# First mixer of a two-trunk network: attention scores emitted in pairs, gate decays interleaved with the last projection jobs, fills in other steps

## What is computed

```python
def trunk_layer(x, cx, c, c_ctx, ...):
    sh1, sc1, ga1, sh2, sc2, ga2 = modulation(c, w_mod, b_mod)       # silu(c) @ w_mod: 1024 x 6144
    u  = (rmsnorm(x,  g_mix) * (1 + sc1)  + sh1)  @ w_in             # 1024 x 2080
    uc = (rmsnorm(cx, g_mix) * (1 + sc1c) + sh1c) @ w_in             # context tokens, 256
    p, gq, gk, gv, gg, rf, rb, aq, ak, av = split_in(u)
    # gated linear attention, both directions, state carried context -> latent
    o_gc, s_f, s_b = gla_bidir(*gla_features(gqc, gkc, gvc, rfc, rbc, ...), 0, 0)
    o_gl, _, _     = gla_bidir(*gla_features(gq, gk, gv, rf, rb, ...), s_f, s_b)
    # softmax attention, 8 query heads of 64, 2 key heads
    #   latent queries see context + latent keys (512), context queries only context (256)
    mix = concat([pool_mixer(p), gla_output(o_gl, gg), latent_attention(ql, k_all, v_all)]) @ w_out
    x = x + ga1 * mix
    x = x + ga2 * squared_relu_mlp(rmsnorm(x) * (1 + sc2) + sh2, w_up, w_down)
    # the same for cx in layer 0 only

def gla_chunk_scan(...):   # the decays: S_new = exp(bl) * S + (k * exp(bl - b))^T v,  b = cumsum(la)
```

## Time and profile before

| what | us |
|---|---|
| median of three runs | 1911.78 |
| lowest, highest | 1906.54, 1918.8 |
| the profiled execution | 1916.42 |
| its span, first to last instruction | 1914.6 |
| mean granted TensorE clock | 0.942 of full |

### The profile page before, as it was taken

One profiled execution on the slowest core, in us unless ns is written; L12 is line 12 of the kernel. 1 busy time (PEld: TensorE's weight loads), 2 busy tenths in 40 slices (PEclk: granted clock), 3 DMA queues, 4 the chain that ended last, 5 costly groups with the idle time before them and its releaser, 6 DMA issues.

```text
span 1914.6 us, 25663 instructions
## 1 busy us (share of the span) xinstructions
PE 1761.6 (92%) x10636; PEld 1411.5 (74%) x10636; DVE 1072.7 (56%) x1634; ACT 704.2 (37%) x878; POOL 84.5 (4%) x87
## 2 busy tenths in 40 slices
PE   4999998899999998999889997987999979779998
PEld 1786456777777777764579995675999766669996
DVE  3664456554444445764566775555666464656654
ACT  2323345321313123433444444363433243633332
POOL 1020000100000001100000001000000010010000
PEclk9999887999999999998989998988999979889999
DMA  9325870224344334258545555431555553335542
GB/s 341 115 104 187 314 271 1 96 86 149 133 149 150 139 132 145 86 182 305 201 152 197 198 181 184 165 132 63 179 177 168 197 202 118 131 110 176 176 168 96
DMA packets 172371, 309.18 MB, mean 161 GB/s; under 512 B 3264, under 2 KB 54720, under 8 KB 171616
## 3 DMA queue, kind: packets, MB, share of 16 engines
q1 hardware_dynamic: 168592, 293.98, 43.8%
q10 hardware_dynamic: 3376, 12.00, 1.8%
q0 software_dynamic: 288, 1.57, 0.2%
HBM read 305.44 MB, written 2.10 MB: 161 GB/s over the span
## 4 chain that ended last, share of the span: by engine, by line
PE 77%; DVE 12%; ACT 4%; DMA 3%; issue 2%; POOL 1%; DVEq 0%; ACTq 0%; POOLq 0%; SPq 0%
PE bank L576 59%; PE twin L576 15%; DVE ring_r L1223 3%; PE bank L585 2%; ACT arena_r L1985 2%; DMA ring<-in_w_in 2%; DMA ring<-in_w_mod 2%; ACT arena L1985 2%; DVE arena L1223 1%; POOL rs L2396 1%; DVE params L1223 1%; DVE arena L1315 1%; DVE arena_r L1223 0%; DVE X L1733 0%; DVE actT_r L1318 0%
## 5 line engine op out<-in xcount | busy, mean ns | idle before, releaser
L576 PE MATMUL bank<-arena_r 128*128 128x512 f32 (+2 forms) x2128 | 702.0, 376 | 14.7 <-DVE arena_r L1855 6.7
L1223 DVE TENSOR_TENSOR ring_r<-ring,arena_r 128x4096 fp32r<-128x4096 f32 (+4 forms) x98 | 394.3, 4023 | 203.6 <-ACT arena_r L1985 202.8
L576 PEld LDWEIGHTS bank<-arena_r 128*128 128x128 f32 x2128 | 405.7, 191 | 94.7 <-issue 8.1
L1985 ACT ACTIVATE arena_r<-ring 128x4096 fp32r<-128x4096 f32 (+4 forms) x96 | 323.5, 3370 | 386.8 <-PE bank L576 129.8
L576 PE MATMUL twin<-actT_r,arena_r 128*128 128x256 f32 x1408 | 254.7, 284 | 1.1 <-DVE actT_r L1223 1.1
L576 PE MATMUL bank<-ring_r,arena_r 128*128 128x512 f32 x624 | 246.1, 394 | 0.0
L576 PE MATMUL bank<-arena_r,actT_r 128*128 128x512 f32 (+3 forms) x624 | 222.0, 387 | 11.9 <-DVE ring_r L1223 5.0
L1985 ACT ACTIVATE arena<-bank 128x512 f32<-128x512 f32 (+6 forms) x195 | 91.8, 471 | 360.8 <-PE bank L576 276.5
L576 PEld LDWEIGHTS twin<-actT_r,arena_r 128*128 128x128 f32 x1408 | 220.1, 192 | 1.7 <-DVE actT_r L1223 1.7
L576 PE MATMUL twin<-actT_r,ring_r 128*128 128x256 f32 x704 | 199.4, 283 | 0.0
L576 PE MATMUL bank<-ring_r,actT_r 128*128 128x512 f32 (+3 forms) x496 | 184.6, 372 | 0.0
(11 more groups left out here) (193 smaller groups left out, 1679.8 us busy)
## 6 DMA issues: line engine op xcount, KB each, us to landing
ring<-in_w_mod SPq DMA_DIRECT2D x24, 2048.0 KB, 9.2
ring<-in_w_ada SPq DMA_DIRECT2D x24, 2048.0 KB, 9.0
ring<-in_w_gate_up SPq DMA_DIRECT2D x44, 1024.0 KB, 7.7
ring<-in_w_down SPq DMA_DIRECT2D x20, 2048.0 KB, 7.9
ring<-in_w_up SPq DMA_DIRECT2D x16, 2048.0 KB, 7.8
ring<-in_w_in SPq DMA_DIRECT2D x12, 2048.0 KB, 11.0
ring<-in_w_out SPq DMA_DIRECT2D x8, 2048.0 KB, 11.2
ring<-in_w_down SPq DMA_DIRECT2D x8, 1792.0 KB, 7.6
```

What stands on the lines that cost most here:

```text
L576: ins = nc.tensor.matmul(out_, lhsT, rhs, start=start, stop=stop)
L1223: return v.tensor_tensor(o, x, y, op)
L1985: return nc.scalar.activation(o, x, func, **kw)
```

## The change

1. **Scores in pairs.** `scores1(l, i)` is called for even i only, and emits the matmuls of steps i and i+1 alternately, into two banks: first the two of head index 0, then, where the range is 256, the two of head index 1. In the loop it stands after `turned1(l, i)` instead of at the head of the step, for even i.
2. **Decays beside the jobs of chunk 4.** `decays(l, tiles)` is called after each of them, with one tile in layer 0 and two in layer 1. The order inside is turned round: the two matmuls of 256 columns first, then the four with one column of that tile. The one-column results go to a bank of ring `s`, and ScalarE takes their exponential after that of the last tile. VectorE multiplies a job later, and waits for ScalarE's last exponential before the mixer.
3. **Fills.** In layer 0 the steps of the fills are 0-5, 7, 8, 9, 11, 12, 13, 15, 17 instead of 0-13; in layer 1 0, 1, 2, 4, 5, 6, 8, 9, 11, 12 instead of 0-5, 8-11. In a step of `WEIGHTED1` the fill comes after `values1`, right ahead of `logs` and `gated_scores`. The number of fills and `loads()` stay. `sums` moves from step 17 to 20 and from 6 to 7. `mod_columns` keeps its steps (`n - 3` is 21 and 13).
4. **Pooling.** The two inner loops change places, so that neighbouring matmuls write different halves of the partitions.

```diff
+def decay_tiles(l, t):
+    return [t] if l < L - 1 else [2 * t, 2 * t + 1]
...
-WEIGHTED1, FILLS1 = [[1, 6, 11, 16], [1, 7]], [range(0, 14), (0, 1, 2, 3, 4, 5, 8, 9, 10, 11)]
-SUMS1, HALVES1 = [17, 6], [20, 12]
+WEIGHTED1 = [[1, 6, 11, 16], [1, 7]]
+FILLS1 = [(0, 1, 2, 3, 4, 5, 7, 8, 9, 11, 12, 13, 15, 17), (0, 1, 2, 4, 5, 6, 8, 9, 11, 12)]
+SUMS1, COLUMNS1, HALVES1 = [20, 7], [21, 13], [20, 12]
...
-            def decays(l):
-                b, filled = take("a")
-                for t in range(4):
-                    for j in range(4):
-                        mm(b[:, 4 * t + j:4 * t + j + 1], la[:, t, j * P:(j + 1) * P], const("up16")[:, P - 1:P],
-                           inc=filled if t == 3 and j == 3 else None)
-                for t in range(4):
+            def decays(l, tiles):
+                if tiles[0] == 0:
+                    pe.wait_ge(la_ready, nth(la_ready))
+                    mark["decs", l] = take("s")
+                whole, whole_filled = mark["decs", l]
+                for t in tiles:
                     b, filled = take("a")
                     mm(b[:, 0:256], const("after16"), la[:, t, 0:256])
                     mm(b[:, 256:512], const("before16"), la[:, t, 256:512], inc=filled)
-                mark["dec", l] = k["a"] - 4
+                    mark["dec", l, t] = k["a"]
+                    for j in range(4):
+                        mm(whole[:, 4 * t + j:4 * t + j + 1], la[:, t, j * P:(j + 1) * P],
+                           const("up16")[:, P - 1:P], inc=whole_filled if t == 3 and j == 3 else None)
...
             def scores1(l, i):
-                heads = steps1(l)[i]
-                b, filled = take("p")
-                for n, (p, e) in enumerate(heads):
-                    t, hp, k0 = pairs1(l)[p]
-                    mm(b[:, 256 * n:256 * n + 512 - k0], qT[64 * e:64 * e + 64, hp, t * P:(t + 1) * P],
-                       kT[64 * e:64 * e + 64, hp // 2, k0:512], inc=filled if n == len(heads) - 1 else None)
+                both = [(s_, take("p")) for s_ in (i, i + 1)]
+                for n in range(len(steps1(l)[i])):
+                    for s_, (b, filled) in both:
+                        heads = steps1(l)[s_]
+                        p, e = heads[n]
+                        t, hp, k0 = pairs1(l)[p]
+                        mm(b[:, 256 * n:256 * n + 512 - k0], qT[64 * e:64 * e + 64, hp, t * P:(t + 1) * P],
+                           kT[64 * e:64 * e + 64, hp // 2, k0:512], inc=filled if n == len(heads) - 1 else None)
...
                 scores1(l, 0)
-                scores1(l, 1)
                 fill()
                 fill()
                 for i in range(n + 1):
-                    if i + 2 < n:
-                        scores1(l, i + 2)
                     if i == 1:
                         pooling(l)
                     if i == 2:
                         pooled(l)
-                    if i in FILLS1[l]:
+                    if i in FILLS1[l] and i not in WEIGHTED1[l]:
                         fill()
                     if i < n:
                         turned1(l, i)
+                    if i % 2 == 0 and i + 2 < n:
+                        scores1(l, i + 2)
                     for p in ended(l, i - 1):
                         values1(l, p)
+                    if i in FILLS1[l] and i in WEIGHTED1[l]:
+                        fill()
...
-                    if j == jobs_until(l, 4):
-                        pe.wait_ge(la_ready, nth(la_ready))
-                        decays(l)
+                    if c == 4:
+                        decays(l, decay_tiles(l, t))
...
-                    if j == jobs_until(l, 4) + 1:
-                        decays(l)
+                    if c == 4 and t > 0:
+                        decays(l, decay_tiles(l, t - 1))
+                decays(l, [3] if l < L - 1 else [2, 3])
+                nth(s_filled)
+                dve.wait_ge(s_emptied, nth(s_emptied))
                 mixer1(l)
```

More of the change, by code:

```diff
@@ L813, in pooling @@
                     for s in range(n // S):
-                        for par_ in range(2):
-                            for t in range(2):
+                        for t in range(2):
+                            for par_ in range(2):
                                 end = s == n // S - 1 and par_ == 1 and t == 1
@@ L911, in mixer1 @@
                             gated_turned(l, t)
-                    if i == n - 3:
+                    if i == COLUMNS1[l]:
                         mod_columns(l + 1)
@@ L1420, in heads, with decays @@
                 dve.wait_ge(a_emptied, mark["qT", l, 1])
-            def decays(l):
+            def decays(l, tiles):
                 ke4 = VIEWS1[l][2]
-                for t in range(4):
-                    dve.wait_ge(a_emptied, mark["dec", l] + 1 + t)
+                for t in tiles:
+                    dve.wait_ge(a_emptied, mark["dec", l, t])
                     for d in range(2):
@@ L1576, in mixer1 @@
                         pooled(l)
-                    if i == n - 2:
+                    if i == COLUMNS1[l] + 1:
                         mod_columns(l + 1)
@@ L2083, in heads, with decays @@
                     step(f(qT[:, j, 0:n], b[:, 0:n], ACT.Copy), a_emptied)
-            def decays(l):
+            def decays(l, tiles):
                 ke4, dec = VIEWS1[l][2], VIEWS1[l][8]
-                b = filled()
-                step(f(dec, b[:, 0:16], ACT.Exp), a_emptied)
-                for t in range(4):
+                for t in tiles:
                     b = filled()
                     step(f(ke4[:, t, :], b[:, :], ACT.Exp), a_emptied)
+                if tiles[-1] == 3:
+                    nth(s_filled, 5)
+                    nth(s_emptied, 5)
+                    b = filled("s")
+                    step(f(dec, b[:, 0:16], ACT.Exp), s_emptied)
             def gated_heads(l):
@@ L2232, in layer1 @@
                     last_c = c
-                    if j == jobs_until(l, 4):
-                        decays(l)
-                nth(s_filled, 5)
-                nth(s_emptied, 5)
+                    if c == 4:
+                        decays(l, decay_tiles(l, t))
                 mixer1(l)
```

## The result

| | before | after |
|---|---|---|
| median of the runs | 1911.9 us (10 runs, 1906.2 to 1918.8) | 1897.8 us (10 runs, 1892.3 to 1903.9) |
| ratio, 95% interval | | 0.9928 [0.9912, 0.9943] |
| span of the profiled execution, its mean clock | 1914.6 us, 0.942 | 1902.1 us, 0.943 |

The change brings 14 us, 0.7%: faster by less than 1%. The prediction said 1894 (1883 to 1908). By the intervals the first set gives 10.9 to 16.8 us and the second 13.6 to 21.8. The forecast sum, 17.9 us, lies above the first and inside the second.

A forecast was written before the change was run, and what follows sets the result against it. TensorE was taken as the bound, busy 92% of the span, with waits and low clock in the mixers. Gains of 7.8 + 5.8 + 4.3 = 17.9 us from a 1911.8 us median gave 1894, range 1883 to 1908.

The forecast's parts named there:

- Decays, 3.9 us a layer: Decays of chunk 4: clock holds, 6.2 us instead of 10.4, less a short wait before `states`; 7.8 us in all.
- The rival that the clock falls all the same: Decays, or `logs` and `states` just after: clock still falls, decays give nothing, 1902 us; chance 0.12.
- Pairs, 1.05 us each: Scores in both mixers: two matmuls run side by side, each pair saving 1.05 us; 19.0 us of work.
- That they don't run side by side: Rival, scores in the loop: only the first pair overlaps, nothing saved and cover lost, 1913 us; chance 0.03.
- The walk of waits: Mixer steps: extra waits where scores no longer cover other engines' chains, 5.7 us in layer 0, 3.25 in layer 1.
- Pooling order, 0.2: Pooling in the mixers: the new order saves the lone first half-pair, 0.2 us a layer.
- Fills' transfers: Weight loads for moved fills in the mixers: no wait expected; otherwise one late landing, 1 to 3 us.
- The 0.4 us of waiting for a chunk in layer 1: First fill with weights issued inside layer 1's mixer: TensorE there at 10.4 us, weights at 10.8.
- Mixer of layer 0, 5.8 us: Layer 0: 11.6 from pairs plus 0.2 pooling less 5.7 of waits is 6.1, taken as 5.8 us gain.
- Mixer of layer 1, 4.3 us: Layer 1: 7.4 from pairs plus 0.2 pooling less 3.25 of waits, a gain of about 4.3 us.
- The clock rival: Both mixers: thinner work is granted less clock, 3.4 us per further low stretch, up to 1931 us; chance 0.04.
- The sign by the clock: Layer 0's mixer: forecast wrong if windows at 0.5 clock total much more or less than about 50 us.

The follow-up runs named there:

- decays_only: The kernel before with the interleaved decays alone, mixers as they were: 1903.1 us, ratio 0.9960 to before.
- lump: The changed kernel with all 16 one-column matmuls of a layer together after the last tile's 256-column matmuls: 1903.6 us, ratio 0.9957 to before.
- old_fills: The changed kernel with fills and sums at their old steps in both layers: 1901.2 us, ratio 0.9932 to before.
- new_fills_layer0: The changed kernel with fills and sums of layer 1 back at their old steps, layer 0 keeping the new: 1896.4 us, ratio 0.9920 to before.
- again: The changed kernel unedited, a second set of six runs with a second profile: 1897.3 us, ratio 0.9908 to before.
- dense_in_waits: The changed kernel plus 16 dense matmuls that nobody reads, put into its mixers' waits: 1894.4 us, ratio 0.9907 to before.
- both: The changed kernel with fills moved into waits and unread dense matmuls in the waits left: 1882.7 us, 0.9856 to before; repeated unchanged 1888.3 us, 0.9879.
- no_pairs: The changed kernel with one score matmul a step at its head, as before; new fills and decays kept: 1906.0 us, ratio 0.9977 to before.

## Why the prediction was right, and where not

The parts of the mechanism were found as forecast: cheaper decays by the clock, the price of a pair, and the places of the waits. That the sum came within 4 us of the median is in part chance, since the mixers' clock moves by several us from one execution to the next, and the sum took it as fixed.

- **Decays, 3.9 us a layer.** From the end of the first job of chunk 4, 139.25, to `logs`, 158.41, before took 19.16 us; after takes 15.55 (141.36 to 156.91). In layer 1 it went from 13.41 us (825.29 to 838.70) to 9.80 (818.30 to 828.10). That is 3.6 a layer, 7.2 in both, and 7.6 by the runs of `decays_only`. The small wait before `states`, forecast at 0.1 to 0.3, does not show as such; there is 0.45 us for VectorE in the middle of `states`, and 0.42 in the same place before. The rival that the clock falls all the same did not come about here, and `lump` shows about what it would have been: 6 us, of which 1.2 are a wait for a bank, against 7.8 in the forecast.
- **Pairs, 1.05 us each.** Right at the full clock, also in steps of 256 columns (267.64 to 268.70, 1.06 us for eight records); at 0.50 such a step takes 2.0 us (279.12 to 281.13). That they don't run side by side is refuted.
- **The walk of waits.** Forecast and measured: step 10 1.7 and 1.94; `gated_scores` of step 11 2.4 and 2.27; the transposes at 15 and 16 2.3 and 2.97, so the gain of 0.4 there did not come; `gated_scores` at 16 0.7 and 0.45; `gated_turned` at 19 2.2 and 2.13; `gated_scores` of layer 1 5.3 and 5.21. In the steps 21 to 24 the waits are 0.48, 2.06, 0.91 and 2.65, against 1.38, 0.90 and 2.65 before: 1.2 more, forecast 1.6. All waits of the mixer of layer 0 went from 10.4 to 17.3 us, 6.9 more, forecast 5.7; in layer 1 from 9.3 to 11.1, 1.8 more, forecast 3.25. In layer 0 this was the best part of the sum: the waits were taken from the lengths of the chain between two events on other engines, and these lengths stayed.
- **Pooling order, 0.2.** Nothing: the 32 records take 3.66 us before and 3.67 after. **Fills' transfers.** The 0.4 us of waiting for a chunk in layer 1 did not come: pooling waits 0.71 us for its bank there before the fill's turn. With the old steps of the fills a wait is there, 0.2 us, and one that I had not foreseen: the fill of step 6 in layer 0 waits 0.97 us for its chunk in `old_fills`. The new steps have no fill there, so of the moved fills about 1 us can be named.
- **Mixer of layer 0, 5.8 us.** The pair of profiles showed 7.05. This agreement is not evidence, since the same old code took 140.3 to 147.6 us and the same new code 134.0 to 141.4.
- **Mixer of layer 1, 4.3 us.** The term that was mis-sized, by the profiles of the kernel: 1.0 and 0.9 measured, though the waits grew by less than forecast. The step that failed is the tacit one that the clock stays as it is, 0.90. It became 0.84, which is 2 x 0.06 x 92 = 11 us more at the half clock, and TensorE's busy time fell by 2.9 us only (83.65 to 80.74), where 7.4 us of work had gone. In the old steps of the fills the term is met, 93.0 to 88.9, but `new_fills_layer0` does not confirm the steps as the cause, and in `lump` the new code meets it too, 93.0 to 88.6 at 0.89. So the term holds where the clock does. What puts the clock down in 865.9 to 873.9 stays open; ahead of it TensorE is in `gated_values`, 24 records of 64 columns without a wait, which take 4.42 us there (from 863.03) and 3.87 in layer 0 (from 192.69).
- **The clock rival.** I gave the stronger fall 0.04 as a case that turns the sign. As a case that takes some microseconds of the gain it came about, in layer 1 of `after` and `again`, and not in that of `lump`. The Trainium skill, in TensorE: Matmul & The Clock Gate, section Part 4: PE-mode transpose, says that a transpose does not count as a busy TensorE in the way of other matmuls. No run here separates them. With dense matmuls in the waits the clock of the mixer of layer 1 is 0.90 (`dense_in_waits`) and 0.98 (`both`, twice); the 0.90 is no more than `lump` has without them.
- **The sign by the clock.** About 50 us at the half clock were forecast for the mixer of layer 0. By the means of its windows it is 2 x 0.14 x 140.6 = 39 us in `after` and 37 in `again`, somewhat less. No wait for a modulation chunk shows in the mixers of `after`.
- **The range.** 1883 to 1908 held both medians of the kernel. It was made of cases; the single times spread with the granted clock.

The sum by the runs: decays 7.6, pairs 8.2 (9 to 13 by `no_pairs`) against 10.1 forecast for both mixers, moved fills not told from nothing, and the measured whole is 13.8 and 17.6.

## What to carry to other kernels

Thin matmuls that stand together can cost beyond their number: spread between dense work a one-column record took 0.10 us, in a row of 32 it took 0.11 to 0.15 in the mean and 0.18 once the clock had fallen, and the work behind them ran slower too. Removing TensorE work that was also cover brought here about half of its length (8 to 13 of 19 us). Putting independent dense work into the waits, moved fills and matmuls that nobody reads together, brought 12 us more. Where the clock is not steady, size nothing from one pair of profiles: profile both kernels twice, and look for the same code in the profiles of the other experiments.

## What the hardware showed that I had not expected

The time of one kernel goes broadly with the mean granted clock of the execution. For nine of the sixteen runs of the kernel after, time and clock:

```
1888.4 0.951    1892.3 0.953    1893.3 0.949    1895.3 0.951
1897.8 0.947    1899.3 0.948    1902.6 0.945    1903.9 0.943    1904.1 0.941
```

A hundredth of mean clock is 2 x 0.01 x 1900 = 38 us at the half clock, and goes with 10 to 12 us of time (a straight line through the sixteen runs of after, and one through the runs of before). So a microsecond at the low clock costs here about 0.3 by this estimate. Part of it lies in waits: the last 8.5 us of the mixer of layer 0 in `after`, at 0.50, have TensorE busy for 5.3. The Trainium skill, in TensorE: Matmul & The Clock Gate, section HAM oscillation, how this bites in real kernels, reckons half of the time at the low clock as lost; the runs here show less. By the mean clocks (0.938 to 0.953) some 180 to 235 of 1900 us are at the half clock in the executions of before and after; in the two profiled ones of `both` it is 160. And a stretch of code may have the low clock in one execution and not in another: the mixer of layer 0 with the same code and the same record counts took 134.0 us at 0.91 and 141.4 at 0.87, and that of layer 1 88.6 at 0.89 and 92.1 at 0.84.
